# Two-block model: the last MLP's down product computed as seven block products with tokens on the partitions

## The reference, cut to what matters

```python
def rmsnorm(x, g):
    y = xf * lax.rsqrt(jnp.mean(xf * xf, axis=-1, keepdims=True) + EPS)
    return (y * g)
def sq_relu_mlp(hn, w1, w2):                  # w1 (1024, 4096), w2 (4096, 1024)
    return jnp.square(jax.nn.relu(hn @ w1)) @ w2
...
        h = h + sq_relu_mlp(rmsnorm(h, norm_mlp_g[l]), mlp_w1[l], mlp_w2[l])
...
    return rmsnorm(h, final_norm_g)
```

## Time and profile before

| what | value |
|---|---|
| times of three runs | 1997.5, 1999.28, 2000.58 us; median 1999.28 |
| the profiled execution's span | 1997.9 us, 1.4 us under the median |
| PE busy | 1979.0 us, 99% |
| DVE, ACT, POOL busy | 1162.7, 765.1, 244.6 us |
| mean granted clock of TensorE | 0.998 of full speed |
| HBM read | 176.91 MB, 90 GB/s over the span |

### The profile page before, as it was taken

How to read it: one execution, slowest core, us unless ns; L and a number is a source line. 1 busy time by engine, 2 the same in 40 slices (tenths; PEclk the granted TensorE clock), 3 DMA queues, 4 the chain that set the end, 5 groups by cost and what they waited for, 6 DMA issues and landing times.

```text
span 1997.9 us, 23010 instructions
## 1 busy us (share of the span) xinstructions
PE 1979.0 (99%) x9333; PEld 1624.3 (81%) x9333; DVE 1162.7 (58%) x1673; ACT 765.1 (38%) x1206; POOL 244.6 (12%) x189
## 2 busy tenths in 40 slices
PE   9999999999999999999999999999999999999998
PEld 7877777888888888888888888888877778888887
DVE  6665687577665656647677444443587674333334
ACT  5453554344333333533324323223554353232224
POOL 1001340000000000000001132221221012222221
PEclk9999999999999999999999999999999999999999
DMA  5322212113232323323222323323232013323321
GB/s 177 108 79 85 85 63 85 64 64 101 89 106 85 106 87 103 106 93 98 87 83 89 106 90 101 104 87 105 74 86 98 24 43 106 105 85 106 103 87 64
DMA packets 138713, 180.51 MB, mean 90 GB/s; under 512 B 9712, under 2 KB 97392, under 8 KB 138608
## 3 DMA queue, kind: packets, MB, share of 16 engines
q1 hardware_dynamic: 136720, 177.52, 27.2%
q10 hardware_dynamic: 1632, 1.51, 0.2%
q0 software_dynamic: 256, 0.02, 0.0%
HBM read 176.91 MB, written 2.10 MB: 90 GB/s over the span
## 4 chain that ended last, share of the span: by engine, by line
PE 94%; DVE 3%; ACT 1%; issue 1%; DMA 0%; POOL 0%; SPq 0%; ACTq 0%; POOLq 0%; DVEq 0%
PE bank L529 26%; PE bank L531 25%; PE bank L530 25%; PE bank L693 4%; PE bank L572 2%; PE bank L574 2%; PE bank L573 2%; PE bank L685 1%; PE bank L783 1%; PE bank L771 1%; PE bank L998 1%; DVE w_lo L1153 1%; DVE arena L1192 1%; PE bank L775 1%; ACT h_hi L1926 0%
## 5 line engine op out<-in xcount | busy, mean ns | idle before, releaser
L529 PE MATMUL bank<-h_hi,w_hi 128*128 128x512 f32 x1384 | 545.7, 394 | 2.0 <-DVE w_lo L1153 2.0
L531 PE MATMUL bank<-h_hi,w_lo 128*128 128x512 f32 x1384 | 539.8, 390 | 0.0
L530 PE MATMUL bank<-h_lo,w_hi 128*128 128x512 f32 x1384 | 539.4, 390 | 0.0
L1911 ACT ACTIVATE w_hi<-raw 128x1024 fp32r<-128x1024 f32 (+2 forms) x335 | 331.1, 1031 | 498.8 <-PE bank L531 442.7
L529 PE MATMUL bank<-g_hi,w_hi 128*128 128x512 f32 (+1 forms) x972 | 377.2, 388 | 1.4 <-issue 0.7
L531 PE MATMUL bank<-g_hi,w_lo 128*128 128x512 f32 (+1 forms) x972 | 371.9, 383 | 0.0
L530 PE MATMUL bank<-g_lo,w_hi 128*128 128x512 f32 (+1 forms) x972 | 371.5, 382 | 0.0
L499 POOL TENSOR_TENSOR w_lo<-raw,w_hi 128x1024 fp32r<-128x1024 f32 (+1 forms) x75 | 182.1, 2429 | 1490.8 <-ACT w_hi L1911 1490.8
L1153 DVE TENSOR_TENSOR w_lo<-raw,w_hi 128x1024 fp32r<-128x1024 f32 (+2 forms) x258 | 309.0, 1221 | 60.8 <-ACT w_hi L1911 59.9
L1215 DVE TENSOR_TENSOR resid<-bank,resid 128x512 f32<-128x512 f32 x287 | 194.3, 688 | 224.9 <-PE bank L531 224.1
L529 PEld LDWEIGHTS bank<-h_hi,w_hi 128*128 128x128 f32 x1384 | 260.3, 188 | 58.4 <-issue 2.8
(11 more groups left out here) (241 smaller groups left out, 1796.0 us busy)
## 6 DMA issues: line engine op xcount, KB each, us to landing
raw<-w SPq DMA_DIRECT2D x64, 1024.0 KB, 5.2
raw<-w_up SPq DMA_DIRECT2D x22, 1024.0 KB, 5.0
raw<-a_w_in SPq DMA_DIRECT2D x16, 1024.0 KB, 5.3
raw<-w_in SPq DMA_DIRECT2D x11, 1024.0 KB, 5.3
raw<-w_down SPq DMA_DIRECT2D x11, 1024.0 KB, 5.0
raw<-w_mkv SPq DMA_DIRECT2D x8, 1024.0 KB, 5.3
raw<-a_w_out SPq DMA_DIRECT2D x8, 1024.0 KB, 5.0
raw<-w_out SPq DMA_DIRECT2D x4, 1024.0 KB, 5.1
```

What stands on the lines that cost most here:

```text
L529: nc.tensor.matmul(dst, a_hi, b_hi, start=(k == 0), stop=False)
L530: nc.tensor.matmul(dst, a_hi, b_lo, start=False, stop=False)
L531: last = nc.tensor.matmul(dst, a_lo, b_hi, start=False, stop=(k == n - 1))
L1911: A(hi, src, ACT.Copy).then_inc(w_hi_done, 1)
```

## The change

The down product of each granule, 512 tokens by 512 hidden features by 1024 outputs, is cut in two in each of its three directions. Of the eight block products seven are made, from sums of blocks (the scheme of Strassen and Winograd, with 4 sums of weight blocks T1 to T4, 4 sums of activation blocks s1 to s4, and sums of the products). The activations are now the stationary operand, so the results have tokens on partitions. P1 and P2 gather over all granules in four PSUM banks of their own; the other five are added on VectorE to float32 sums in SBUF. The last granule keeps P6 and P7 in the banks of P1 as well.

Weights of this MLP leave the shared ring. They are split in pieces of 1024 elements through a ring of four pieces, 11 to a granule: 4 for the up product, and 7 forms of `w2`. ScalarE makes all highs (`high_piece`), VectorE all lows (`low_piece`). GpSimd makes no lows here, but the sums T1 to T4 (1024 elements each) and s1 to s4 (2 x 256 each).

The residual is turned to tokens by 32 transposes in granules 1 to 4. The 32 transposes at the end go, and so does the sum of squares on TensorE: ScalarE squares with a running sum. The final gain is multiplied in by GpSimd on half of the output and by VectorE on the other half, and the store is eight DMAs of 256 KB.

The core of the diff:

```diff
-    out += mlp("w1_1", "w2_1")
...
+        PRODUCTS = ("P1", "P2", "P6", "P4", "P7", "P5", "P3")
+        A_GRANULE = 4 + len(PRODUCTS)
+        FORM_OF = {"P1": "B11", "P2": "B21", "P6": "T2", "P4": "T4", "P7": "T3", "P5": "T1", "P3": "B22"}
+        LEFT_OF = {"P1": (slice(0, 2), 0), "P2": (slice(2, 4), 0), "P6": (slice(0, 2), 0), "P4": (slice(2, 4), 256),
+                   "P7": (slice(0, 2), 256), "P5": (slice(2, 4), 0), "P3": (slice(0, 2), 0)}
...
+        def jobs_of(n):
+            return TURN_JOBS[2 * n - 2:2 * n] if 1 <= n <= 4 else []
+
+        def is_kept(n, product):
+            return product in KEPT or (n == GRANULES - 1 and product in ("P6", "P7"))
...
+        last_tiles, kept_done, USED_BY = 0, 0, []
+        for n in range(GRANULES):
+            for jobs in (len(jobs_of(n)), 0):
+                last_tiles += 2
+                USED_BY += [(tile_full, last_tiles)] * 2
...
+            for n in range(GRANULES):
+                for half in range(2):
+                    if n:
+                        wait_lows(sp, A_GRANULE * (n - 1) + 10 + half)
+                    sp.dma_start(quarter_view(quarters, half), down_rows[:, 4 * n:4 * n + 4, 512 * half:512 * half + 512])\
+                      .then_inc(quarter_loaded[half], 16)
+                for i in range(2):
+                    if n < GRANULES - 1:
+                        wait_lows(sp, A_GRANULE * n + 2 * i + 2)
+                        load_up(2 * n + 2 + i)
...
+            b11, b21, b12, b22 = [quarters[:, j // 2, 1024 * (j % 2):1024 * (j % 2) + 1024] for j in range(4)]
+            a11, a21 = [last_g[:, 0:2, 256 * t:256 * t + 256] for t in range(2)]
+            a12, a22 = [last_g[:, 2:4, 256 * t:256 * t + 256] for t in range(2)]
+            s1, s2, s3, s4 = [last_s[:, j, :].rearrange("p (k n) -> p k n", k=2) for j in range(4)]
+            for n in range(GRANULES):
+                p = A_GRANULE * n
+                wait_lows(pool, p + 5)
+                pool.wait_ge(quarter_loaded[1], 16 * (n + 1))
+                G.tensor_tensor(b11, b12, b11, ALU.subtract).then_inc(form_made, 1)
+                pool.wait_ge(form_made, 4 * n + 1)
+                G.tensor_tensor(second_form, b22, b11, ALU.subtract).then_inc(form_made, 1)
+                wait_lows(pool, p + 6)
+                pool.wait_ge(form_made, 4 * n + 2)
+                G.tensor_tensor(b21, second_form, b21, ALU.subtract).then_inc(form_made, 1)
+                pool.wait_ge(g_made, 4 * n + 2)
+                pool.wait_ge(left_ready, 7 * n)
+                G.tensor_tensor(s3, a11, a21, ALU.subtract).then_inc(left_made, 1)
+                G.tensor_tensor(b12, b22, b12, ALU.subtract).then_inc(form_made, 1)
+                pool.wait_ge(left_made, 4 * n + 1)
+                pool.wait_ge(g_made, 4 * n + 4)
+                G.tensor_tensor(s2, a22, s3, ALU.subtract).then_inc(left_made, 1)
+                G.tensor_tensor(s1, a21, a22, ALU.add).then_inc(left_made, 1)
+                pool.wait_ge(left_made, 4 * n + 2)
...
+            for j, y in enumerate([turned_first[:, t, :] for t in range(2)] + [sums["P4"][:, t, :] for t in range(2)]):
+                pool.wait_ge(y_squared, j + 1)
+                G.tensor_tensor(y, y, first_half, ALU.mult).then_inc(y_gained, 1)
 
...
+            def last_up(n, i):
+
+                p = A_GRANULE * n + 2 * i
+                wait_lows(pe, p + 2)
+                halves = [[ring(t, p + j).rearrange("p (k n) -> p k n", n=COLS) for j in range(2)] for t in (w_hi, w_lo)]
...
+            def product(n, j):
+
+                name = PRODUCTS[j]
+                p = A_GRANULE * n + 4 + j
+                wait_lows(pe, p + 1)
+                pe.wait_ge(left_ready, 7 * n + (1, 3, 4, 5, 5, 6, 7)[j])
+                b_hi, b_lo = [ring(t, p).rearrange("p (k n) -> p k n", k=2) for t in (w_hi, w_lo)]
...
+                ends = n == GRANULES - 1
...
+                opens = n == 0 if kept else True
+                for t in range(2):
+                    dst = (on[t] if kept else next_bank())[:]
+                    cut = slice(P * t, P * t + P)
+                    for k in range(2):
+                        begin = opens and k == 0
+                        nc.tensor.matmul(dst, a_hi[:, k, cut], b_hi[:, k, :], start=begin, stop=False, skip_group_check=kept)
+                        nc.tensor.matmul(dst, a_hi[:, k, cut], b_lo[:, k, :], start=False, stop=False, skip_group_check=kept)
+                        last = nc.tensor.matmul(dst, a_lo[:, k, cut], b_hi[:, k, :], start=False,
+                                                stop=k == 1 and (ends or not kept), skip_group_check=kept)
...
+                    last.then_inc(kept_full, 1)
...
+            for n in range(GRANULES):
+                last_up(n, 0)
+                for half, t in jobs_of(n):
+                    turn_tokens(half, t)
+                last_up(n, 1)
+                for j in range(len(PRODUCTS)):
+                    product(n, j)
...
+            def low_piece(p):
+                dve.wait_ge(w_hi_done, PIECES * OLD + p + 1)
+                V.tensor_tensor(ring(w_lo, p), form_source(p), ring(w_hi, p).bitcast(F32), ALU.subtract).then_inc(w_split, 1)
...
+            def low_left(name, src, n_hi):
+                dve.wait_ge(left_hi, n_hi)
+                V.tensor_tensor(left_form(g_lo, name), src, left_form(g_hi, name).bitcast(F32), ALU.subtract)\
+                 .then_inc(left_ready, 1)
...
+            for n in range(GRANULES):
+                p, hi = A_GRANULE * n, 8 * n
+                ends = n == GRANULES - 1
+                rectified(0)
+                rectified(1)
+                low_piece(p + 4)
+                low_piece(p + 5)
+                low_left("P1", last_g[:, 0:2, 0:256], hi + 2)
+                for half, t in jobs_of(n):
+                    take_tokens(half, t)
+                if ends:
+                    together(sums["P7"], sums["P7"], sums["P6"], ALU.add)
+                    together(sums["P3"], sums["P3"], sums["P6"], ALU.add)
+                rectified(2)
+                low_left("P7", left_sum(2), hi + 3)
+                if ends:
+                    together(sums["P4"], sums["P7"], sums["P4"], ALU.subtract)
+                    together(sums["P3"], sums["P3"], sums["P5"], ALU.add)
+                    together(turned_last, turned_last, sums["P7"], ALU.add)
+                    together(turned_last, turned_last, sums["P5"], ALU.add)
+                rectified(3)
+                low_left("P2", last_g[:, 2:4, 0:256], hi + 5)
+                low_piece(p + 6)
+                low_left("P6", left_sum(1), hi + 6)
+                if ends:
+                    break
+                low_left("P4", last_g[:, 2:4, 256:512], hi + 5)
+                low_piece(p + 7)
+                take_product(n, "P6", 0)
+                low_piece(p + 8)
+                take_product(n, "P6", 1)
+                low_left("P5", left_sum(0), hi + 7)
+                take_product(n, "P4", 0)
+                low_piece(p + 9)
+                take_product(n, "P4", 1)
+                take_product(n, "P7", 0)
+                low_left("P3", left_sum(3), hi + 8)
+                take_product(n, "P7", 1)
+                low_piece(p + 10)
+                take_product(n, "P5", 0)
+                low_piece(p + 11)
+                low_piece(p + 12)
+                take_product(n, "P5", 1)
+                take_product(n, "P3", 0)
+                low_piece(p + 13)
+                take_product(n, "P3", 1)
+                low_piece(p + 14)
...
+            first_kept = 2 * (GRANULES - 1)
+            dve.wait_ge(kept_full, first_kept + 1)
+            settle()
+            keep_order(V.tensor_tensor(turned_first[:, 0, :], KEPT["P1"][0][:], turned_first[:, 0, :], ALU.add))
+            V.tensor_tensor(turned_first[:, 1, :], KEPT["P1"][1][:], turned_first[:, 1, :], ALU.add).then_inc(kept_taken, 1)
...
+                    act.wait_ge(form_made, 4 * n + {"T1": 1, "T2": 2, "T4": 3, "T3": 4}[FORM_OF[PRODUCTS[j - 4]]])
+                else:
+                    half = int(FORM_OF[PRODUCTS[j - 4]] == "B22")
+                    act.wait_ge(quarter_loaded[half], 16 * (n + 1))
+                if p < 4:
+                    act.wait_ge(tile_full, ENDS[OLD - 2 + (OLD + p // 2) % 2])
+                else:
+                    wait_used(act, p - 4, start_last)
+                A(ring(w_hi, p), form_source(p), ACT.Copy).then_inc(w_hi_done, 1)
...
+            high_piece(2)
+            high_piece(3)
+            root(rstd[:, 0, :], None, stat_bank[:], None, D)
+            for n in range(GRANULES):
+                p = A_GRANULE * n
+                if n:
+                    act.wait_ge(left_made, 4 * n)
+                square_tile(0)
+                high_piece(p + 4)
+                square_tile(1)
+                high_piece(p + 5)
+                act.wait_ge(left_made, 4 * n + 1)
+                high_left("P7", 2)
+                tile.n += len(jobs_of(n))
```

(99 more changed lines are left out.)

251 lines of the change are left out of this document (153 added, 98 removed).

## The result

| kernel | median of its runs | lowest to highest | ratio to before, 95% interval |
|---|---|---|---|
| before | 1999.28 us | 1997.5 to 2000.58 | |
| after | 2046.13 us | 2044.83 to 2046.58 | 1.0233 [1.0219, 1.0248] |

The changed kernel is 2.3% slower; 2048 us was predicted. Its profiled execution has a span of 2044.1 us, against 1997.9 before.

What follows compares the result with a forecast made beforehand. TensorE, busy 99% of the span, was taken as the bound. Terms of -21.8+3.6-0.2+28.5+9.1+12.6+4.8+11.6+0.5 = +48.7 us on a 1997.9 span gave 2046.6, hence a median of 2048 us, range 2018 to 2070.

Steps and rivals of the forecast that it cites:

- wait before P2, granules 1 to 4: TensorE's wait for P2's low, 4.45 us in each; with 5.35 in granules 5 and 6, +28.5 us.
- first granule: TensorE's wait before P2 in the first granule: P2 ready at 1672.1, wanted at 1663.0, +9.1 us.
- Mutual blocking: Before P2, VectorE instructions with two SBUF inputs and GpSimd instructions reading SBUF exclude each other throughout; part of +28.5 us.
- Prices: GpSimd's sums before P2: 2.4 us for a T sum starting at once, 2.3 after waiting, 1.3 for s3.
- rival of fast sums: GpSimd's float32 block sums take VectorE's time, 1.15 us for 1024 elements: 1995 us, chance 0.07.
- the one of costly strided sums: s1 to s4 take 2.49 us each instead of 1.3, making P2 and P6 later: 2082 us, chance 0.06.
- no blocking: VectorE's lows slip in beside GpSimd, leaving waits of 1.3 and 0.4 us before P2: 2002 us, chance 0.07.
- The list of turns: Engine steps in written order from piece p+4 to P2's low, ending 29.85 us after the granule's start.
- The clock: After the wait before P2, TensorE runs at a slow clock, losing 1.65 us in seven granules: +11.6 us.
- U+4.4 against U+4.25: U is P2's start: P2 ends at U+4.4 us at the slow clock, P6's low is ready at U+4.25.
- the bound of 2036 without any clock loss: Forecast for the whole kernel if the clock stays at 2.4 GHz after the waits: 2036 us.
- The last granule: Six sums in VectorE's list, +12.6 us before P2; then 21.1 us to the last matmul, not 16.3, +4.8.

Runs made afterwards that it cites:

- e6: e5 with the last granule's six product sums moved to its start and s1 held on GpSimd until P6's low is made: 1994.83 us.
- e2: Changed kernel with GpSimd's four weight-block sums each replaced by two memsets that only write, s1 to s4 kept: 2010.86 us.
- e3: Changed kernel plus 18 unused matmuls into a spare bank between P1 and P2 of each granule: 2040.20 us.
- e1: Changed kernel with GpSimd making T3 behind s2 instead of right behind s3: 2045.99 us.
- e7: e6 with s2 also held on GpSimd until VectorE has made P2's low: 1999.14 us.
- e8: e7 with the third tile's two squares each split into halves of 256 columns, left halves first: 1995.47 us.
- e9: e8 with the low of P3's weight piece moved ahead of the second addition of P7 in VectorE's list: 1994.12 us.
- e5: Changed kernel with T1, T4 and T3 in buffers of their own and all four T sums made at the granule's start: 2005.88 us.

## Why the prediction was right

Right in mechanism and place; its terms against the trace (the profiled span is 2.5 us under the predicted 2046.6):

| term | predicted | measured |
|---|---|---|
| wait before P2, granules 1 to 4 | 4.45 | 4.05 to 4.07 |
| the same, 5 and 6 | 5.35 | 4.94 |
| first granule | 9.1 | 6.62, and 1.50 before P1 |
| last granule, before P2 | 12.6 | 11.80 |
| last granule, P2's start to the last matmul | 21.1 | 18.9 (2013.27 to 2032.17) |
| period, 1 to 6 | 47.9 | 47.53 to 47.94 |
| transposes, a granule | 0.9 | 0.92 (e6: 42.79 less 41.87) |
| last matmul to the end | 11.2 | 11.9 |

The waits are as listed; each costs 0.16 more, so the true distance to the prediction is that much smaller.

- *Mutual blocking* was the step that carried the forecast. Lows of 3.00, 2.88 and 2.20 beside T sums, and 1.23, 0.69 and 0.69 beside memsets (e2), show it. The Trainium skill, SBUF — State Buffer, "Who interferes with whom", says that a VectorE instruction with two SBUF inputs contends with a GpSimd one that reads SBUF and not with one that only writes. The trace of after agrees with the first half (3.00 beside T1), e2 with the second (1.23 beside memsets).
- *Prices.* T sums of 2.39 and 2.40 where nothing was in the way (predicted 2.4), s3 1.29 (1.3). The rival of fast sums is out by these rows, the one of costly strided sums by s3 and by s2's 1.26; no blocking by the lows.
- *The list of turns* gave P2's low at 29.85 after the granule's start. From T1's start, predicted 13.5, to that low's end it is 16.35; the trace has 1846.98 to 1862.89, 15.91, 0.4 less, in keeping with the shorter wait.
- *The clock* fell as said: nine matmuls in 3.58 us instead of 2.04, 1.54 lost. As a price of its own it was mis-sized. The prediction set it beside P6's low (U+4.4 against U+4.25) and added it in full. e3 shows that without it P6's low makes TensorE wait instead, so only 0.4 of 1.65 per granule, some 3 of 11.6 us, would come back; the bound of 2036 without any clock loss was too low (e3: 2040.20). The sum was still right, since in the kernel as it is the slow stretch stands on the path. The rule of the Trainium skill, TensorE: Matmul & The Clock Gate, "HAM oscillation — how this bites in real kernels", that a wait in each tile of work makes each one start slow, agrees with all eight waits before P2 in after (PEclk 0.50 to 0.59 in the 4 us behind each). It does not with e1, where four waits of 2.54 to 3.44 before P2 were followed by 1.00.
- *The last granule* was mis-sized by 0.8 and 2.2 us, the largest error: after P2, TensorE waited only once (0.36 on VectorE's addition) where three waits were expected. The end was too short by 0.7. I did not follow either further.

What was expected of undoing parts was too good six times. In e1, e7, e8 and e9 the next step in VectorE's list was taken to have slack, where it had little or none; in e1 the clock added to it. In e5 waits were counted as listed, without what a restart and the clock cost; in e6 the transposes were counted as cover.

## What to carry to other kernels

Fewer matmuls pay only if what feeds them is early: here 21.8 us of matmuls were saved by block sums that held up the lows behind them, and TensorE waited 44.5. Put a GpSimd instruction that reads SBUF where the two-input VectorE work has none to do, not where it is merely short: moving the sums to the idle stretch gave back 38 us, moving one of them (T3) among the same lows gave none. And before pricing the removal of a wait, ask which step stands next in the same list and by how much it is early.

## What the runs showed of the hardware

- In the granule shown the two engines took turns by whole instructions: T1, the low of p+5, T2, the low of P1, T4, each ending its own time (2.25 to 2.4, 1.1, 0.55) after the other engine's last. The recorded duration of a held-up instruction contains its wait.
- A GpSimd memset of 128x1024 float32 took 0.95 us, a two-input sum of the same size 2.39.
- The same wait leaves the clock low in some executions and not in others. Windows of 1480 to 1490 us, ahead of every change, in after and in e3: the same 8.02 us busy, PEclk 0.83 and 1.00.

```profile
1480.00:1490.00 10.00, 8.02 (x29) 6.17 (x28) 9.70 (x14) 6.49 (x12) 3.17 (x2) 0.83 0.26 61
```

```profile
1480.00:1490.00 10.00, 8.02 (x40) 6.39 (x38) 9.74 (x15) 6.33 (x11) 2.03 (x2) 1.00 0.24 61
```

- In e1 the 2.55 us wait at 1766.44 was followed by full clock and the 2.56 us wait at 1814.78 by PEclk 0.63 (1815 to 1818); what decides it stays open.
